# Second attention of a two-block model: query tiles of a head pair joined into items of 512 score columns

## The reference

```python
def masked_softmax(s, mask):
    p = jax.nn.softmax(jnp.where(mask, s, NEG), axis=-1)
    return jnp.where(mask, p, 0.0)
# for every branch b, with its keys k_b, values v_b and gate g_b:
#   out += g_b * (masked_softmax(q @ k_b.T, mask_b) @ v_b)
```

## Time and profile before

| | us |
|---|---|
| median of 3 runs | 1687.8 |
| lowest, highest | 1687.55, 1687.91 |
| span of the profiled execution | 1686.5 |
| TensorE busy in it | 1666.9 (99%) |
| VectorE, ScalarE, GpSimd busy | 882.4, 386.9, 211.3 |
| second attention, first scores to the first output part behind it | 126.2 |

### The profile page before, as it was taken

One profiled execution on the slowest core, in us unless ns is written; L12 is line 12 of the kernel. 1 busy time (PEld: TensorE's weight loads), 2 busy tenths in 40 slices (PEclk: granted clock), 3 DMA queues, 4 the chain that ended last, 5 costly groups with the idle time before them and its releaser, 6 DMA issues.

```text
span 1686.5 us, 20192 instructions
## 1 busy us (share of the span) xinstructions
PE 1666.9 (99%) x7754; PEld 1007.8 (60%) x7754; DVE 882.4 (52%) x1509; ACT 386.9 (23%) x702; POOL 211.3 (13%) x279
## 2 busy tenths in 40 slices
PE   9999999999999999999999999999999999999999
PEld 5887888885433343433334455688855544667664
DVE  3755746765433232323225446676756654677663
ACT  3122212002100000000002212321245524544530
POOL 2333310001100000000001000010235420000000
PEclk9999999999999999999999999999999999999999
DMA  7313113244899999999995123114120021212101
GB/s 282 125 59 117 51 58 127 100 197 190 330 423 426 427 426 426 428 426 428 427 427 237 50 75 125 51 63 164 63 101 1 1 76 57 94 51 78 72 1 50
DMA packets 28003, 308.14 MB, mean 183 GB/s; under 512 B 4415, under 2 KB 4703, under 8 KB 10112
## 3 DMA queue, kind: packets, MB, share of 16 engines
q1 hardware_dynamic: 21456, 288.70, 42.2%
q0 software_dynamic: 6448, 18.10, 3.1%
HBM read 306.06 MB, written 4.19 MB: 184 GB/s over the span
## 4 chain that ended last, share of the span: by engine, by line
PE 92%; DVE 4%; DMA 2%; ACT 1%; issue 1%; POOL 0%; DVEq 0%; SPq 0%; ACTq 0%
PE ps L442 87%; PE ps L445 4%; DVE arena L1270 2%; DMA wring<-in_w 2%; ACT arena L2508 1%; DVE arena L1297 0%; DVE arena L1281 0%; DMA H<-in_x 0%; DVE small L1285 0%; POOL small L2948 0%; ACT HT L2508 0%; DVE arena L1275 0%; DVE wring L1270 0%; DVE H L1270 0%; DVE arena L1354 0%
## 5 line engine op out<-in xcount | busy, mean ns | idle before, releaser
L442 PE MATMUL ps<-arena 128*64 128x512 f32 (+13 forms) x2484 | 534.0, 395 | 4.3 <-DVE arena L1293 1.2
L442 PEld LDWEIGHTS ps<-arena 128*64 128x64 f32 (+4 forms) x2484 | 249.3, 156 | 223.0 <-issue 211.7
L442 PE MATMUL ps<-wring,arena 128*64 128x512 f32 (+2 forms) x1048 | 345.1, 564 | 0.0
L1270 DVE TENSOR_TENSOR arena<-ps,arena 128x512 f32<-128x512 f32 (+1 forms) x196 | 134.1, 684 | 382.1 <-PE ps L442 229.3
L442 PE MATMUL ps<-wring,HT 128*128 128x512 f32 (+1 forms) x880 | 311.2, 505 | 4.9 <-ACT HT L2508 3.3
L442 PEld LDWEIGHTS ps<-wring,HT 128*128 128x128 f32 x880 | 163.4, 190 | 125.8 <-issue 112.2
L442 PE MATMUL ps<-HT,wring 128*128 128x512 f32 (+2 forms) x656 | 222.1, 501 | 0.0
L2508 ACT ACTIVATE arena<-ps 128x512 f32<-128x512 f32 (+4 forms) x155 | 82.8, 534 | 593.9 <-PE ps L445 304.2
L442 PE MATMUL ps<-wring 128*128 128x256 f32 x864 | 195.7, 380 | 0.0
L442 PEld LDWEIGHTS ps<-wring,arena 128*64 128x64 f32 (+1 forms) x1048 | 131.3, 151 | 87.4 <-issue 82.6
L1270 DVE TENSOR_TENSOR H<-ps,H 128x512 f32<-128x512 f32 x182 | 125.8, 691 | 97.6 <-PE ps L442 96.0
(11 more groups left out here) (125 smaller groups left out, 1008.1 us busy)
## 6 DMA issues: line engine op xcount, KB each, us to landing
wring<-in_w SPq DMA_DIRECT2D x47, 2048.0 KB, 22.1
wring<-in_dense SPq DMA_DIRECT2D x38, 2048.0 KB, 8.4
arena<-in_w SPq DMA_DIRECT2D x35, 2048.0 KB, 19.5
HT<-in_w SPq DMA_DIRECT2D x12, 2048.0 KB, 18.9
arena<-in_rows POOLq DMA_DIRECT2D x29, 256.0 KB, 4.0
wring<-in_dense SPq DMA_DIRECT2D x2, 1024.0 KB, 6.1
H<-in_x SPq DMA_DIRECT2D x4, 512.0 KB, 7.3
arena<-in_relb POOLq DMA_DIRECT2D x8, 256.0 KB, 8.5
```

Source lines behind the costliest of these rows:

```text
L442: return nc.tensor.matmul(o, l, r, start=start, stop=stop, skip_group_check=True)
L1270: done(nc.vector.tensor_tensor(o, a, b, op), tell)
```

## The change

`items_d` now makes six items of a pair. Behind kind 0 come five items of 512 columns of scores, each a list of parts (kind, q): (1, 3); (2, 3); (1, 2) with (1, 0), 384 + 128 columns; (2, 2) with (2, 0); (1, 1) with (2, 1), 256 + 256. A part has an offset o in the item's bank and buffers. The number of items is 24 instead of 36. Scores, minima, exponentials and scalings are still done for each part, with the counters y of its own for sums and minima (16 columns for the minima instead of 8). Done once an item are: the wait for a free bank, the turns of both banks, the two copies of the turned probabilities, and GpSimd's wait and its operation for the reciprocals, of four columns where there are two parts. A bank of scores is handed on when both its parts are written and freed when both are read. The quota of the filler goes from 0.56 to 0.81 an item. GpSimd's `weigh` is split in two: `weigh_a` is what the first attention did before, and `weigh_d` is for the second.

```diff
             for hh in range(4):
                 yield dict(hh=hh, kind=0, last=False)
-                for kind in (1, 2):
-                    for q in (3, 0, 2, 1):
-                        yield dict(hh=hh, kind=kind, q=q, nk=128 * (q + 1), last=(kind, q) == (2, 1))
+                for parts in (((1, 3),), ((2, 3),), ((1, 2), (1, 0)), ((2, 2), (2, 0)), ((1, 1), (2, 1))):
+                    o, own = 0, []
+                    for kind, q in parts:
+                        own.append(dict(kind=kind, q=q, o=o, nk=128 * (q + 1)))
+                        o += 128 * (q + 1)
+                    yield dict(hh=hh, kind=3, parts=own, nk=o, last=parts[0] == (1, 1))
...
-                               lambda g: {"e0": 2, "e1": 1}[g[0]], 0.56, NIT + 3, 4)
+                               lambda g: {"e0": 2, "e1": 1}[g[0]], 0.81, NIT + 3, 4)
...
-                    for u in range(2):
-                        f = F["sd", it["x"] + u]
-                        mm(f.ap[:, 0:it["nk"]], q_of(hh, u, it["q"]),
-                           nkT[64 * u:64 * u + 64, gg + (2 if it["kind"] == 2 else 0), 0:it["nk"]]).then_inc(f.full, 1)
+                    for part in it["parts"]:
+                        o, nk = part["o"], part["nk"]
+                        for u in range(2):
+                            f = F["sd", it["x"] + u]
+                            ins = mm(f.ap[:, o:o + nk], q_of(hh, u, part["q"]),
+                                     nkT[64 * u:64 * u + 64, gg + (2 if part["kind"] == 2 else 0), 0:nk])
+                            if part is it["parts"][-1]:
+                                ins.then_inc(f.full, 1)
...
-                            ttr(pD[x % 6][:, 0:nk], f.ap[:, 0:nk], causal[:, 512 - nk:], small[:, 176 + x % 8:177 + x % 8], f)
+                            for part in it["parts"]:
+                                o, nk, low = part["o"], part["nk"], 176 + (part["y"] + u) % 16
+                                ttr(pD[x % 6][:, o:o + nk], f.ap[:, o:o + nk], causal[:, 512 - nk:], small[:, low:low + 1],
+                                    f if part is it["parts"][-1] else "v")
...
-                            p = pD[x % 6][:, 0:it["nk"]]
-                            act(p, p, ACT.Exp, "ed", scale=-1.0, bias=small[:, 176 + x % 8:177 + x % 8],
-                                accum_out=sums[:, x:x + 1])
+                            for part in it["parts"]:
+                                y, low = part["y"] + u, 176 + (part["y"] + u) % 16
+                                p = pD[x % 6][:, part["o"]:part["o"] + part["nk"]]
+                                act(p, p, ACT.Exp, "ed", scale=-1.0, bias=small[:, low:low + 1], accum_out=sums[:, y:y + 1])
...
+            def weigh_d(it):
+
+                y, n = it["parts"][0]["y"], 2 * len(it["parts"])
+                g.wait_ge(S("ed"), saw("ed", n))
+                nc.gpsimd.tensor_tensor(rcp[:, y:y + n], sums[:, y:y + n], C("mone").to_broadcast([128, n]),
+                                        ALU.pow).then_inc(S("g"), 1)
+                g.wait_ge(S("g"), told("g"))
+                for u in range(2):
+                    for part in it["parts"]:
+                        p = pD[(it["x"] + u) % 6][:, part["o"]:part["o"] + part["nk"]]
+                        r, k = rcp[:, part["y"] + u:part["y"] + u + 1], 6 * it["hh"] + 3 * u + part["kind"]
+                        ins = nc.gpsimd.tensor_scalar(p, p, r, gates[:, part["q"], k:k + 1], MUL, MUL)
+                    ins.then_inc(S("pd"), 1)
```

More of the change, by code:

```diff
@@ L414, in build @@
         NIT = len(ITEMS)
-        _x = 0
+        _x = _y = 0
         for it in ITEMS:
             it["x"] = _x
-            _x += 2 * (it["kind"] > 0)
+            if it["kind"]:
+                _x += 2
+                for part in it["parts"]:
+                    part["y"] = _y
+                    _y += 2
         sumsA, rcpA = small[:, 80:112], small[:, 112:144]
@@ L649, in turn_probs @@
                         pe.wait_ge(S("pd"), saw("pd"))
-                        for c in range(it["q"] + 1):
+                        for c in range(it["nk"] // 128):
                             ins = tr(f.ap[:, c * 128:c * 128 + 128], pD[x % 6][:, c * 128:c * 128 + 128])
@@ L661, in values @@
                         return
-                    f, q, x = F["yT2", hh], it["q"], it["x"]
-                    c0 = (128 if it["kind"] == 1 else 384) + 64 * gg
+                    f, x = F["yT2", hh], it["x"]
                     evacuated(("pt", "D", x), ("pt", "D", x + 1))
[L665 to L668, removed]
+                    for part in it["parts"]:
+                        q, o = part["q"], part["o"]
+                        c0 = (128 if part["kind"] == 1 else 384) + 64 * gg
+                        for c in range(q + 1):
+                            for u in range(2):
+                                ins = mm(f.ap[64 * u:64 * u + 64, q * 128:q * 128 + 128], kv4[:, c, c0:c0 + 64],
+                                         ptD[(x + u) % 4][:, o + c * 128:o + c * 128 + 128], False,
+                                         it["last"] and part["kind"] == 2 and c == q)
                     if it["last"]:
@@ L2199, in lows @@
                     if it["kind"]:
-                        nk = it["nk"]
-                        for x in (it["x"], it["x"] + 1):
+                        for u in range(2):
+                            x = it["x"] + u
                             f = full("sd", x)
@@ L2970, in weigh @@
                 for u in range(2):
[L2971 to L2976, removed]
+                    p, r = pA[(x + u) % 6][:, 0:n], rcpA[:, x + u:x + u + 1]
+                    nc.gpsimd.tensor_scalar(p, p, r, None, MUL).then_inc(S("pa"), 1)
+            def weigh_d(it):
[4 more added lines that the diff above has]
+                g.wait_ge(S("g"), told("g"))
+                for u in range(2):
+                    for part in it["parts"]:
+                        p = pD[(it["x"] + u) % 6][:, part["o"]:part["o"] + part["nk"]]
+                        r, k = rcp[:, part["y"] + u:part["y"] + u + 1], 6 * it["hh"] + 3 * u + part["kind"]
+                        ins = nc.gpsimd.tensor_scalar(p, p, r, gates[:, part["q"], k:k + 1], MUL, MUL)
+                    ins.then_inc(S("pd"), 1)
             def bias(h):
@@ L3069, in gpsimd @@
             for it in ITEMS:
[L3070 to L3073, removed]
+                if it["kind"]:
+                    weigh_d(it)
             f = F["yT2", 3]
```

12 lines of the change are left out of this document (7 added, 5 removed).

## The result

| | before | after |
|---|---|---|
| median of the runs, us | 1687.86 | 1677.55 |
| lowest to highest | 1687.55 to 1689.64 | 1677.14 to 1678.04 |
| ratio, 95% interval | | 0.9935 (0.9923 to 0.9947) |
| span of the profiled execution | 1686.5 | 1675.4 |
| second attention, first scores to first output part | 126.14 | 114.95 |

The changed kernel is faster by 0.65%, 10.3 us by the medians and 11.1 by the spans. The forecast was a gain of 8.0 us, 1679.8, and its range ended at 1677.3. The median by itself, 1677.55, lies just inside that end. By the ratio, which compares it with the kernel before timed beside it, it lies 11 us under the time before (1687.8 x 0.9935 = 1676.8), just outside. Either way the direction was right and the gain was taken too small. In a later set of runs the changed kernel was timed again: 1677.1, ratio 0.9931 (0.9918 to 0.9945).

What follows compares the result with a forecast made beforehand. TensorE's own sequence was taken to bound the second attention, busy 121.93 of 126.17 us. Terms -3.7 (groups) - 4.8 (waits) + 0.5 (new waits) = -8.0 took 1687.8 to 1679.8 us, range 1677.3 to 1683.8.

Steps and rivals of the forecast that it cites:

- groups of turns and values, 12 fewer: TensorE, second attention: size-independent costs of 12 turn and value groups fall away, 0.31 us each pair of groups, 3.7 us.
- groups of scores, 12 fewer: TensorE, second attention: each pair of score matmuls pays its own changeover, so joining scores gives nothing, zero.
- waits that go: TensorE, second attention: waits ahead of turns for VectorE's and ScalarE's copies go, with short gaps and excess, 4.8 us.
- new waits: TensorE, second attention: 0.4 us in the tight places and 0.1 in the tail, 0.5 us (0 to 2.5).
- part 2: Cost of a group on TensorE: turns and values save 3.7 us (3.4 to 4.0), joined scores zero.
- the tight place: Step after the compressed scores: VectorE needs 4.0 to 4.9 us against TensorE's 4.9; 0.1 us a pair allowed.
- the chain: Joined item's probabilities, minima to scalings: 7.4 us, hidden under TensorE's 8.0 or more, by 0.6 at the least.
- rival C: Second attention: joined scores share changeovers, some 0.1 for each of two passes, 12 items, 2.4 us: 1677.4; chance 0.10.
- A: Second attention: group costs go, waits mostly stay or move to the tight step; -3.7 to -5.2, 1683.4 us; chance 0.14.
- D: Second attention: joined scores cost more than apart, row halves out of step, 0.3 an item, 3.6 us, 1683.4; chance 0.09.
- B: Joined item's chain exceeds two steps, TensorE waits ahead of 12 items' turns; at 1.0 an item +4.0, 1691.8; chance 0.05.

Runs made afterwards that it cites:

- the experiment: Changed kernel with, for scores, first parts of joined items' scores issued earlier: 1680.72 us; for turns, second head's turns issued behind filler and values: 1681.59 us.
- the pieces of 128 columns: Changed kernel with every score matmul of the causal branches cut into matmuls of 128 columns, 96 more passes: 1678.27 us, ratio 0.994.
- the third bank: Kernel before with three banks for turns instead of two in the second attention, the filler with one instead of two: 1686.86 us, ratio 0.9994.

## Why the prediction fell short, point by point

| term, us | forecast | measured |
|---|---|---|
| groups of turns and values, 12 fewer | -3.7 | -4.0 |
| groups of scores, 12 fewer | 0 | -2.3 |
| waits that go | -4.8 | -5.0 |
| new waits | +0.5 | +0.1 |
| the stage | -8.0 | -11.2 |

Measured are the stage and the waits. The 6.3 us left over are the groups. By the experiment the scores have 12 x 0.19 = 2.3 of it, and 4.0 are left for turns and values together. The 3.2 us by which the sum fell short are 2.3 of scores, 0.3 of turns and values, 0.2 of old waits and 0.4 of new ones.

**The step that failed** is in part 2: "Each pair pays its own changeover within one group, so joining scores gives nothing: I take zero." It took the time of a pair with 31 columns, 0.12 or more, for a changeover, because a turn of 128 columns lasts no longer. The row was read rightly and its cause was guessed: a second cause, a floor below which a pass doesn't go however few its columns, fits the row as well, and the pieces of 128 columns settle for it. The trace of before had what would have decided. A pair of 128 columns and a pair of 384 apart take 0.42 and 0.85, so 256 columns more cost 0.43, 1.7 ns a column for the two passes; 128 columns are then 0.21, and 0.2 of the 0.42 is the group. Part 2 made just this subtraction for turns and for values and not for scores. What the Trainium skill, "TensorEngine Tiling (Array Packing)", section "Key Properties", says, that a change of mode drains and a change of tile within it doesn't, was set aside because of that row. The runs here agree with it: 96 passes more within a group cost 6 ns each, a 64*128 group more costs 0.19 us beside its columns.

**Turns and values** (3.7 against 4.0): right in mechanism and nearly in size. The turns' group was 0.14 in the forecast and in the experiment. For the values' group the 0.15 that was taken holds: read matmul by matmul, sixteen take 1.02 us from start to start, eight 0.59 and four, with scores behind them, 0.37; the four with 0.40 in the earlier trace rows were 0.02 above that, which gave the 0.19. The 0.3 that is left isn't tied to one kind of group; a turn group costs less beside a filler (below), and how many stand so changed as well: 13 of 32 had no filler beside them before, 5 of 20 after.

**The waits** (4.8 against 5.0): right in size and, by the third bank, in cause. The excess over the idle time was needed: 3.4 of idle time stood for 5.0. Why they go, TensorE's larger step against VectorE's, fits the timelines but wasn't tested apart: a step of the changed kernel has larger groups and also more filler, and no run has the one without the other.

**New waits** (0.5 against 0.1): the tight place has one wait of 0.04 us in four pairs, and the chain was overrated twice. It is shorter than worked out, and its cover is longer. GpSimd's and VectorE's timelines for the item scored at 1244.81:

```profile
1246.11 0.56 DVE L1368 CUSTOM_DVE_ANT_0 arena<-ps,arena 128x384 f32<-128x384 f32 x1
```

```profile
1249.69 1.02 POOL L2997 TENSOR_TENSOR arena<-arena,con 128x4 f32<-128x4 f32 x1 [2.26 <-ACT arena L2525]
1250.81 2.16 POOL L3004 TENSOR_SCALAR arena<-arena 128x384 f32<-128x384 f32 x4
```

```profile
1255.37 1.09 PE L452 MATMUL ps<-con,arena 128*128 128x128 f32 x8
```

First minimum to last scaling is 1246.11 to 1252.97, 6.9 us where 7.4 were worked out; the reciprocals of four took 1.02, the forecast's slope. From its scores to its turns are 10.6 us, not 8.0, so all its probabilities lie ready 2.4 us early. All other joined items but the last two have 2.3 to 2.8 us too. The margin is small only in the last steps: 1.3 us for the last item but one, and for the last, whose scalings end at 1340.75 and whose turns begin at 1341.48, 0.7.

**What the profile was to show:** eight turns 1.0 us (1.03), waits for copies under 0.6 (0.04), 330 us behind (330.09), the clock at 1.00, all as said; idle of 1 to 1.5 came out at 0.88, and 118 us at 114.95. The sign written down for rival C, a span that falls by 10, is what came: 11.1. C had 2.4 us for the scores, and 2.3 is what they gave; the other 0.9 by which the stage beat the forecast is no part of C.

**The other rivals:** A is out, since no wait on the copies is left. D is out: joined scores take 1.07 where apart they take 1.27. B is a real mechanism, but the chain has more room than it said: it had the whole gain gone with the chain 1.3 us longer, and with 1.0 more the stage loses 0.9 us altogether, in the last pair alone; with 3.0 more it loses 24.

## What to carry to other kernels

Cost every kind of group by the same subtraction, two groups of different length of the same kind, before deciding that one of them has no fixed cost; a per-instruction time that doesn't fall with the size is as likely a floor as a changeover. Where TensorE is busy 97% of a stage, the number of its groups still is time: 0.5 us for each item of scores, turns and values that falls away, in a stage with waits and in one without. Here the waits went with steps made longer on the engine that sets the pace, at nearly the same work on the others, while another bank alone only moved them.

## What the runs showed of the hardware

- A pass of two concurrent 64-row matmuls has a floor of 0.11 us: 31 and 128 columns take the same time, and from 128 to 384 the columns are paid.
- A group costs 0.14 to 0.15 (turns), 0.15 (values) and 0.19 to 0.20 us (scores) beside its columns. Turns next to filler matmuls, both on the whole array, cost 0.1 less: in the changed kernel the eight turns at 1245.88 are followed by a filler after 0.93 us, the eight at 1341.48 by values after 1.03.
- After a wait of 2.72 us, then four turns and a wait of 0.62 more, TensorE's clock went down: in the windows above 1.00 ahead of it, 0.54 in the two microseconds from 1302, near the lower of its two levels (1.2 GHz), and 1.00 again from 1304 on. Four filler matmuls took 3.03 us there, where the earlier trace rows have 1.88. The same came behind the waits of 2.77 and 3.79 us, and behind none of 1.1 or less that stood alone. The three stretches cost about 1.6 us each, on top of the waits of 2.7 to 3.8 us themselves.
